# Gated one-hot rows for eight tokens: eight narrow comparison-and-product operations, or one wide comparison and one wide product

## The chip, the cores and the metric

The kernel runs on one core of a Trainium2 chip. The metric is the device time of one execution in microseconds. A core has TensorE (matmuls), VectorE, ScalarE and GpSimd (elementwise work, each with its own queue of instructions), and SyncE, whose queue issues most of the DMA transfers. The engines wait for each other through semaphores.

## The reference, cut to what matters

The program is two transformer blocks in a row, each over two layers and 256 tokens of width 1024. The first block ends each layer with a mixture of 16384 small experts. An expert has a number of two parts, `i1 * 128 + i2`, and each token picks 8 heads x 16 experts, with a softmax gate for each:

```python
eidx = jnp.take_along_axis(cidx, pos, axis=-1)       # 8 x 16 experts of each token
gate = jax.nn.softmax(top, axis=-1).astype(h.dtype)
u = expert_u[ec]
act = jax.nn.gelu(jnp.einsum('td,thkd->thk', hc, u), approximate=False)
return jnp.einsum('thk,thkd->td', gc * act, expert_v[ec])
```

## The kernel before

The kernel does not gather experts. It streams all of them and weights each token's activation of each expert by a gate, which is zero for those that the token did not pick. For that it needs a table `G` of gates: for each token a 128 x 128 matrix, first key by second key. The table is built in the loop that is changed here.

For one token, the 128 picks lie across the partitions of `pairsT`: `pairsT[:, 0]` is one part of the expert's number, `pairsT[:, 1]` the other, `pairsT[:, 2]` the gate, each with one column for a token. `iota` holds 0 to 127 along the free dimension of every partition. Comparing `iota` with a pick's part gives a one-hot row of 128. The product of the plain one-hot rows (part 1) and the gated ones (part 0, multiplied by the gate), summed over the 128 picks by one matmul, is the token's 128 x 128 gate matrix.

Tokens go in groups of `TOKG = 8`, 32 groups in each of two layers. `rows` holds two groups, `[:, n % 2, 0]` gated and `[:, n % 2, 1]` plain, all f32 in SBUF. For a group n:

- VectorE (L2328 to L2337) makes the eight gated rows, one `tensor_scalar` each, which compares and multiplies (L2331), and the last of the plain rows (L2335), and signals `gated_rows`.
- GpSimd (L1947 to L1953) makes four plain rows (L1951) and signals `plain_rows`.
- ScalarE (`one_hot`, L1650 to L1657) makes three plain rows as relu(1 - (key - iota)^2): three squares (L1653), a drain, one relu over all three (L1655), and signals `act_rows`.
- TensorE (L1126 to L1134) waits for the three signals, and for the copy of group n - 2, then multiplies eight times (L1132) into one half of `gate_ps` and signals `gates_full`.
- ScalarE (`gates_out`, L1661 to L1663) copies the group's gates from PSUM to `G` and signals `gates_kept`. Its order is rows of group n + 1, then the copy of group n.

VectorE, GpSimd and ScalarE each begin the rows of group n when TensorE has finished group n - 2 (`gates_full.two_before`), since its buffer is then free. After the loop the experts are streamed, which needs the whole of `G`. In the first layer VectorE runs L2322, a subtraction of two SBUF tensors of 2048 elements per partition, just before the loop, when GpSimd has already begun its rows. Other lines that are read below: L1392 and L1400 belong to the picking of the keys ahead of the loop (`pick_keys`, on VectorE and on GpSimd), L1408 and L2314 to L2318 to the softmax of the gates, L1930 to the inverse roots of the norms, L2013 to a norm, and L2344 to the stream of experts.

Of the kernel before, what the change touches and what calls it, by code (L numbers as in the profile page):

```python
# [11 lines left out]
ALU = mybir.AluOpType  # L12
# [3 lines left out]
P = 128  # L16
# [16 lines left out]
TOKG = 8  # L33
# [114 lines left out]
def spread(ap, axis, n):  # L148

    v = ap.unsqueeze(axis)  # L150
    shape = list(v.shape)
    shape[axis] = n
    return v.broadcast_to(shape)
# [65 lines left out]
def two_blocks(nc, io, out):  # L219
    ctx = ExitStack()  # L220
    with ctx:
        def sem(name):
            return ctx.enter_context(nc.semaphore(name))

        def sb(name, shape, dt=F32):
            return ctx.enter_context(nc.sbuf_tensor(name, shape, dt))
# [57 lines left out]
        gated_rows = Signal(sem("gated_rows"), a=S // TOKG)  # L284
# [41 lines left out]
        iota = sb("iota", [P, P])  # L326
# [110 lines left out]
        rows = rs.take(2, 2, TOKG, P)  # L437
        rp = Region(arena, NKEYS * S + D + 2 * S + 2 * KD * S)
        pairsT = rp.take(3, S)
# [77 lines left out]
        def acc_nat(b, n=512):  # L517

            return acc[:, b].rearrange("p (t x) s -> p t (x s)", t=2)[:, :, 0:n]
# [1440 lines left out]
        def _(dve_):  # L1960
            dve = nc.vector
# [192 lines left out]
            for l in range(DEPTH):  # L2154
# [171 lines left out]

                for n in range(S // TOKG):
                    dve.wait_ge(*gates_full.two_before("a", l, n + 1))  # L2328
                    for q in range(TOKG):
                        tok = n * TOKG + q  # L2330
                        dve.tensor_scalar(rows[:, n % 2, 0, q, :], iota[:], pairsT[:, 0, tok:tok + 1],  # L2331
                                          pairsT[:, 2, tok:tok + 1], ALU.is_equal, ALU.mult)
                    for q in range(POOLQ + ACTQ, TOKG):
                        tok = n * TOKG + q
                        ins = dve.tensor_scalar(rows[:, n % 2, 1, q, :], iota[:], pairsT[:, 1, tok:tok + 1], None,  # L2335
                                                ALU.is_equal)
                    ins.then_inc(gated_rows.sem, 1)  # L2337

                dve.wait_ge(*gates_kept.at("a", l, S // TOKG))

# [82 lines left out]
            for l in range(DEPTH):  # L2423
# [45 lines left out]
                for t in range(T):  # L2469
                    ins = dve.scalar_tensor_tensor(bt2[:, t], cc[:, t, 0:QR], rstd[:, t:t + 1], cqg, ALU.mult, ALU.mult)  # L2470
                ins.then_inc(qk_ready.sem, 1)
                for t in range(T):
                    ins = dve.scalar_tensor_tensor(bt[:, t, 0:KVR], cc[:, t, QR:QR + KVR], rstd[:, T + t:T + t + 1], ckvg,
                                                   ALU.mult, ALU.mult)
# [15 lines left out]
                for t in range(T):  # L2490
                    ins = dve.tensor_tensor(oh[:, t], oh[:, t], spread(subln, 1, DH), ALU.mult)
# [20 lines left out]
                for t in range(T):  # L2512
                    dve.tensor_copy(kf4[:, t, :, 0:NOPE], kv4[:, t, :, 0:NOPE])
                    ins = dve.tensor_copy(kf4[:, t, :, NOPE:LQ], spread(cc[:, t, 384:416], 1, LH))
# [18 lines left out]
                for c in range(NB):  # L2533
                    for n in range(GC):
# [6 lines left out]
                        for t in range(T):  # L2541
                            ins = dve.scalar_tensor_tensor(bt[:, t], gcol[:, t], 1.0, acc_nat(accs.buf("b", use))[:, t],
                                                           ALU.add, ALU.mult)
                        ins.then_inc(accs.free_sem("b", use), 1)
                        dve.drain()
                        for t in range(T):
                            if c == 0:
                                ins = dve.tensor_scalar(bn[:, t, cols], bt[:, t], 0.5, None, ALU.mult)
                            else:
                                ins = dve.scalar_tensor_tensor(bn[:, t, cols], bt[:, t], 0.5, bn[:, t, cols], ALU.mult, ALU.add)  # L2550
# [167 lines left out]
```

## Time and profile before

| what | value |
|---|---|
| median of 3 runs | 3237.7 us (3234.63 to 3239.08) |
| the profiled execution, its own time | 3236.21 us |
| its span, first to last instruction | 3234.3 us |
| busy: TensorE matmul, VectorE, ScalarE, GpSimd | 92%, 60%, 39%, 8% of the span |
| mean granted TensorE clock | 0.959 |
| the changed loop, layer 0 | VectorE's first operation at 294.3 us, TensorE's last eight matmuls end at 380.2 us |
| the changed loop, layer 1 | 1389.96 us to 1475.9 us |

Shares of the span are averages over stages with different limits; the loop is about 170 us of it. An idle engine costs time only where the next thing waits for it. The granted clock is 1 at TensorE's full level (2.4 GHz) and 0.5 at the lower one (1.2 GHz); a value between them is a mixture over the stretch.

### The profile page before, as it was taken

Reading aid. Unit: us, or ns where it says so; the run is one execution under the profiler, and the core shown is the slowest. Engines: PE = TensorE matmul, PEld = TensorE weight load, DVE = VectorE, ACT = ScalarE, POOL = GpSimd, SP = SyncE. Lnnn points to the kernel's source line nnn. Section 1 sums busy time; section 2 is a strip of 40 time slices with the busy share of each in tenths; the row PEclk is TensorE's granted clock in tenths of the full one; section 3 lists DMA queues with packets and bytes.
Section 4 is the critical chain, followed back from the end, with each engine's and each line's share of the span. In section 5 each row is a group of like instructions: output and inputs, shape, how many; then the busy total and the mean of one; then the engine's idle time right before and its main releaser. Section 6 shows DMA issues by size and latency. Waiting matters only on the chain.

```text
span 3234.3 us, 48577 instructions
## 1 busy us (share of the span) xinstructions
PE 2989.4 (92%) x17170; PEld 2544.4 (79%) x17170; DVE 1949.9 (60%) x3622; ACT 1276.4 (39%) x2037; POOL 274.2 (8%) x387
## 2 busy tenths in 40 slices
PE   8897899999999888968999999998999898999898
PEld 4574798999999765867999999987874887975597
DVE  4659856777777632897666666655542654543464
ACT  0235744444444311575444444434430433431243
POOL 0027600000000000572000000000000000000000
PEclk9899999999999988989999999998999999999899
DMA  8432155666666531304555555544332454323353
GB/s 314 181 118 79 43 189 205 228 229 233 230 225 231 189 122 52 118 1 142 184 188 188 193 196 190 194 158 178 114 142 104 158 188 165 119 117 124 130 183 143
DMA packets 130819, 524.25 MB, mean 162 GB/s; under 512 B 17997, under 2 KB 28109, under 8 KB 108041
## 3 DMA queue, kind: packets, MB, share of 16 engines
q1 hardware_dynamic: 120664, 508.13, 44.5%
q10 hardware_dynamic: 10034, 14.52, 1.3%
q8 instruction: 74, 1.21, 0.2%
q14 instruction: 47, 0.39, 0.0%
HBM read 519.44 MB, written 3.16 MB: 162 GB/s over the span
## 4 chain that ended last, share of the span: by engine, by line
PE 77%; issue 8%; ACT 6%; DVE 6%; DVEq 1%; ACTq 1%; DMA 1%; POOL 0%; PEldq 0%; SPq 0%; POOLq 0%; PEld 0%
PE prob_ps L1149 22%; PE acc L1160 21%; PE acc L858 7%; PE acc L798 4%; PE acc L843 3%; PE acc L819 3%; PE acc L1341 3%; PE acc L1356 3%; PE acc L1317 3%; ACT arena L1663 2%; PE turn_ps L926 2%; PE turn_ps L871 1%; PE acc L900 1%; ACT arena L1653 1%; ACT slab L1655 1%
## 5 line engine op out<-in xcount | busy, mean ns | idle before, releaser
L1149 PEld LDWEIGHTS prob_ps<-hTr,utr 128*128 128x128 f32 x5952 | 749.2, 192 | 33.1 <-issue 15.0
L1149 PE MATMUL prob_ps<-hTr,utr 128*128 128x256 f32 x5952 | 760.4, 284 | 8.3 <-DVE arena L2392 3.5
L1160 PE MATMUL acc<-vr,wtr 128*128 128x512 f32 x3024 | 736.4, 392 | 5.2 <-DVE vr L2369 5.2
L1160 PEld LDWEIGHTS acc<-vr,wtr 128*128 128x128 f32 x3024 | 553.8, 189 | 111.4 <-issue 6.4
L2369 DVE TENSOR_TENSOR vr<-slab,vr 128x1024 fp32r<-128x1024 f32 x252 | 308.7, 1225 | 418.1 <-ACT vr L1697 418.0
L1697 ACT CAST vr<-slab 128x1024 fp32r<-128x1024 f32 x252 | 264.5, 1050 | 586.7 <-PE acc L1160 584.1
L2344 DVE TENSOR_TENSOR utr<-slab,utr 128x1024 fp32r<-128x1024 f32 x248 | 302.0, 1218 | 14.0 <-ACT utr L1680 14.0
L1680 ACT CAST utr<-slab 128x1024 fp32r<-128x1024 f32 x248 | 259.3, 1046 | 9.5 <-issue 4.9
L1930 POOL TENSOR_TENSOR small<-small 128x2 f32<-128x2 f32 (+3 forms) x18 | 24.4, 1355 | 2798.3 <-DVE small L2002 1488.2
L2583 DVE TENSOR_TENSOR slab_lo<-slab,w_hi 128x2048 fp32r<-128x2048 f32 x64 | 143.8, 2288 | 126.2 <-ACT w_hi L1903 126.2
L1687 ACT ACTIVATE arena<-prob_ps 128x256 f32<-128x256 f32 x248 | 95.4, 385 | 225.3 <-PE prob_ps L1149 225.3
L1903 ACT CAST w_hi<-slab 128x2048 fp32r<-128x2048 f32 x64 | 119.3, 1906 | 164.8 <-DMA slab<-in_pack_b 151.6
L2431 DVE TENSOR_TENSOR slab_r<-slab,arena_r 128x2048 fp32r<-128x2048 f32 (+1 forms) x52 | 115.7, 2258 | 110.3 <-ACT arena_r L1777 86.8
L1132 PE MATMUL acc<-slab 128*128 128x128 f32 x1024 | 133.9, 286 | 41.2 <-ACT slab L1655 30.6
L1132 PEld LDWEIGHTS acc<-slab 128*128 128x128 f32 x1024 | 123.9, 198 | 51.5 <-DVE slab L2335 41.9
L819 PE MATMUL acc<-hT,slab 128*128 128x256 f32 x704 | 159.2, 386 | 1.7 <-issue 1.7
L1356 PE MATMUL acc<-w_hi,uTr 128*128 128x512 f32 x512 | 157.9, 390 | 2.5 <-issue 2.3
L1951 POOL TENSOR_SCALAR slab<-iota,arena 128x128 f32<-128x128 f32 x256 | 153.9, 616 | 45.1 <-ACT arena L1377 29.2
L2331 DVE TENSOR_SCALAR slab<-iota,arena 128x128 f32<-128x128 f32 x512 | 152.5, 367 | 3.6 <-PE acc L1132 3.4
L819 PEld LDWEIGHTS acc<-hT,slab 128*128 128x128 f32 x704 | 135.6, 194 | 22.3 <-issue 3.7
L871 PE MATMUL turn_ps<-ident,arena 128*128 128x128 f32 (+1 forms) x336 | 68.2, 365 | 91.8 <-ACT arena L1757 41.6
L871 PEld LDWEIGHTS turn_ps<-ident,arena 128*128 128x128 f32 (+1 forms) x336 | 51.9, 185 | 113.4 <-ACT arena L1757 33.4
(272 smaller groups left out, 4054.1 us busy)
## 6 DMA issues: line engine op xcount, KB each, us to landing
slab<-in_pack_b SPq DMA_DIRECT2D x132, 1024.0 KB, 4.8
slab<-in_peer_v SPq DMA_DIRECT2D x256, 512.0 KB, 3.5
slab<-in_peer_u SPq DMA_DIRECT2D x248, 512.0 KB, 4.7
arena<-in_pack_a SPq DMA_DIRECT2D x84, 512.0 KB, 5.4
slab<-in_pack_a SPq DMA_DIRECT2D x40, 1024.0 KB, 6.8
arena<-in_peer_u SPq DMA_DIRECT2D x4, 1024.0 KB, 13.0
slab<-in_pack_b SPq DMA_DIRECT2D x4, 832.0 KB, 5.3
arena<-in_pack_a SPq DMA_DIRECT2D x2, 1024.0 KB, 18.7
```

The costliest lines, as they stand in the source:

```text
L819: ins = pe.matmul(dst, w(k, a, P), lhs[:, k, :], start=(k == 0), stop=(k == KD - 1))
L858: ins = pe.matmul(dst[:, t, 0:n], hT_r[hp][:, 4 * h + k, t * P:t * P + P], proj_operand(u0 + h, wp)[:, k, a:a + n], start=(h == 0 and k == ...
L1132: ins = pe.matmul(gate_ps[:, n % 2, q * P:q * P + P], rows[:, n % 2, 1, q, :], rows[:, n % 2, 0, q, :], start=True, stop=True)
L1149: ins = pe.matmul(prob_ps[:, m % 2, 0:S], utr[:, m % 2, uh, k * P:k * P + P], hTr[:, hh, k, :], start=(k == 0 and n == 0), stop=(k == KD - ...
L1160: ins = pe.matmul(y_ps[:, t, n, :], wtr[:, m % 2, wh, t * P:t * P + P], v_place(l, i)[:, vh, n * 512:n * 512 + 512], start=first and k == ...
L1356: ins = pe.matmul(dst[:, t, :], uTr[:, up, 4 * j + k, t * P:t * P + P], mlp_operand(u, wp)[:, k, :], start=(j == 0 and k == 0 and m == 0), ...
L1680: act.copy(utr[:, m % 2, 0], expert_u[:, m % 2]).then_inc(ut_act.sem, 1)
L1697: act.copy(v_place(l, i)[:, 0], expert_v[:, m % 2]).then_inc(v_hi.sem, 1)
L1951: ins = nc.gpsimd.tensor_scalar(rows[:, n % 2, 1, q, :], iota[:], pairsT[:, 1, tok:tok + 1], None, ALU.is_equal)
L2331: dve.tensor_scalar(rows[:, n % 2, 0, q, :], iota[:], pairsT[:, 0, tok:tok + 1], pairsT[:, 2, tok:tok + 1], ALU.is_equal, ALU.mult)
L2344: dve.tensor_tensor(utr[:, m % 2, 1], expert_u[:, m % 2], utr[:, m % 2, 0].bitcast(F32), ALU.subtract).then_inc(ut_dve.sem, 1)
L2369: dve.tensor_tensor(v_hl[:, 1], expert_v[:, m % 2], v_hl[:, 0].bitcast(F32), ALU.subtract)\
```

## The change

VectorE makes the eight gated rows of a group with two operations in place of eight. The first compares 8 x 128 elements: the picks' parts of eight tokens, each repeated 128 times, with `iota`, repeated eight times. `spread` makes a view with a step of zero along one axis; nothing is copied. The second multiplies the result in place with the eight gates, each repeated 128 times. Between the two stand the one plain row of VectorE, as before, and a drain. The signal `gated_rows` moves from L2335 to the product. GpSimd's, ScalarE's and TensorE's parts are unchanged.

```diff
                 for n in range(S // TOKG):
                     dve.wait_ge(*gates_full.two_before("a", l, n + 1))
-                    for q in range(TOKG):
-                        tok = n * TOKG + q
-                        dve.tensor_scalar(rows[:, n % 2, 0, q, :], iota[:], pairsT[:, 0, tok:tok + 1],
-                                          pairsT[:, 2, tok:tok + 1], ALU.is_equal, ALU.mult)
+                    first, gated = n * TOKG, rows[:, n % 2, 0]
+                    dve.tensor_tensor(gated, spread(pairsT[:, 0, first:first + TOKG], 2, P), spread(iota[:], 1, TOKG),
+                                      ALU.is_equal)
                     for q in range(POOLQ + ACTQ, TOKG):
-                        tok = n * TOKG + q
-                        ins = dve.tensor_scalar(rows[:, n % 2, 1, q, :], iota[:], pairsT[:, 1, tok:tok + 1], None,
-                                                ALU.is_equal)
-                    ins.then_inc(gated_rows.sem, 1)
+                        tok = first + q
+                        dve.tensor_scalar(rows[:, n % 2, 1, q, :], iota[:], pairsT[:, 1, tok:tok + 1], None, ALU.is_equal)
+                    dve.drain()
+                    dve.tensor_tensor(gated, gated, spread(pairsT[:, 2, first:first + TOKG], 2, P), ALU.mult)\
+                        .then_inc(gated_rows.sem, 1)
```

## Rows read from the trace of the kernel before

**Rows 1.** The page: busy time of each engine over the span.
```profile
PE 2989.4 (92%) x17170; PEld 2544.4 (79%) x17170; DVE 1949.9 (60%) x3622; ACT 1276.4 (39%) x2037; POOL 274.2 (8%) x387
```

**Rows 2.** Windows: us busy of PE, PEld, DVE, ACT, POOL; granted clock, DMA share, GB/s.
```profile
294.00:300.00 6.00, 2.92 (x14) 2.95 (x15) 5.16 (x19) 1.21 (x4) 4.19 (x7) 0.50 0.00 0
300.00:310.00 10.00, 8.36 (x61) 7.88 (x61) 9.12 (x33) 8.40 (x17) 8.37 (x15) 0.89 0.01 2
320.00:340.00 20.00, 15.71 (x126) 14.42 (x125) 20.00 (x72) 18.85 (x41) 18.55 (x32) 1.00 0.01 2
1380.00:1390.00 10.00, 1.80 (x6) 1.00 (x6) 8.02 (x17) 0.69 (x2) 0.40 (x1) 0.54 0.00 1
```

**Rows 3.** Timeline of one group: start, length, engine, line, operation, idle before it.
```profile
326.17 0.52 ACT L1655 ACTIVATE slab<-arena 128x384 f32<-128x384 f32 x1
326.20 0.31 DVE L2335 TENSOR_SCALAR slab<-iota,arena 128x128 f32<-128x128 f32 x1
326.45 2.39 DVE L2331 TENSOR_SCALAR slab<-iota,arena 128x128 f32<-128x128 f32 x8
326.62 2.38 POOL L1951 TENSOR_SCALAR slab<-iota,arena 128x128 f32<-128x128 f32 x4 [0.18 <-PE acc L1132]
...
326.95 2.02 PE L1132 MATMUL acc<-slab 128*128 128x128 f32 x16 [0.54 <-ACT slab L1655]
...
328.76 0.31 DVE L2335 TENSOR_SCALAR slab<-iota,arena 128x128 f32<-128x128 f32 x1
329.01 0.34 DVE L2331 TENSOR_SCALAR slab<-iota,arena 128x128 f32<-128x128 f32 x1
```

**Rows 4.** The chain that ended last, one turn of it in the loop.
```profile
313.97 1.01 ACT arena L1663
...
315.93 0.52 ACT slab L1655
...
316.53 1.01 ACT arena L1663
```

**Rows 5.** Waits from 304 to 378 us, and L1951 by itself (least, median, most).
```profile
PE acc L1132 <- ACT slab L1655: 15.3, 28, 0.8
...
L1951 POOL TENSOR_SCALAR slab<-iota,arena x256: 592/597/2542, 291.5 to 1472.7; 128x128 f32<-128x128 f32 x128
```

**Rows 6.** Groups of VectorE by form: count, busy time, mean ns.
```profile
L2344 DVE TENSOR_TENSOR utr<-slab,utr 128x1024 fp32r<-128x1024 f32 x248 | 302.0, 1218 | 14.0 <-ACT utr L1680 14.0
L1392 DVE TENSOR_TENSOR arena<-arena,small 128x512 f32<-128x512 f32 x8 | 5.2, 693 | 0.3
```

**Rows 7.** Timeline of VectorE: around a drain, and nine operations in a row.
```profile
289.81 0.41 DVE L2314 TENSOR_REDUCE small<-arena 128x16 f32<-128x256 f32 x1
290.30 0.25 DVE L2316 RECIPROCAL small<-small 128x16 f32<-128x16 f32 x1
...
296.80 2.26 DVE L2331 TENSOR_SCALAR slab<-iota,arena 128x128 f32<-128x128 f32 x8
```

**Rows 8.** Timeline where VectorE and GpSimd meet, and GpSimd's L1930 alone.
```profile
272.55 3.27 DVE L1400 TENSOR_TENSOR arena<-arena 128x512 f32<-128x512 f32 x2
273.56 1.71 POOL L1400 TENSOR_TENSOR arena<-arena 128x512 f32<-128x512 f32 x1
291.92 2.28 DVE L2322 TENSOR_TENSOR hTr<-hT,hTr 128x2048 fp32r<-128x2048 f32 x1
292.13 2.54 POOL L1951 TENSOR_SCALAR slab<-iota,arena 128x128 f32<-128x128 f32 x1
1270.98 0.69 POOL L1930 TENSOR_TENSOR small<-small 128x2 f32<-128x2 f32 x1 [91.68 <-DVE small L2000]
2189.54 1.22 DVE L2013 TENSOR_TENSOR arena<-x,arena 128x1024 f32<-128x1024 f32 x1
2189.72 1.62 POOL L1930 TENSOR_TENSOR small<-small 128x2 f32<-128x2 f32 x1 [716.41 <-DVE small L2002]
```

**Rows 9.** The chain that ended last, at the loop's first group.
```profile
297.08 3.77 PE acc L1132 x16
```

## The prediction

> **What bounds the kernel now.** I read the page first. Matmuls run through 92% of the span and VectorE through 60% [rows 1], so an edit to VectorE's work should matter only in a stage where TensorE waits. The edited loop is such a stage: it runs for 32 groups of eight tokens in each of two layers, and the next stage needs all of its output. The stretches [rows 2] show what the reader should look for: in the middle of the loop TensorE is busy 15.7 of 20 us, while VectorE is busy 20.00, ScalarE 18.85 and GpSimd 18.55. Three engines are nearly full, so which of them sets the pace has to be read from one group.
>
> The timeline of one group [rows 3] repeats every 2.56 us (VectorE's first narrow operation of a group starts at 326.45, of the next at 329.01). ScalarE goes copy, three squares, relu, and the copy again without waiting. VectorE does its nine operations in 2.56 us. GpSimd does four in 2.38 us and waits 0.18 us. TensorE needs 2.02 us and waits 0.54 us for ScalarE's relu: that ended at 326.69 (326.17 + 0.52), VectorE's last operation of the same group at 326.51, and TensorE began at 326.95. The chain of waits says the same [rows 4]: it stays on ScalarE, from a copy at 313.97 over the relu at 315.93 to the next copy at 316.53, 2.56 us, and touches neither VectorE nor GpSimd. The waits of the stage [rows 5] agree: 28 waits of TensorE for ScalarE's L1655 in 74 us. So ScalarE sets 2.56 us by itself; VectorE ends 0.18 us ahead of it, and GpSimd's 0.18 us of waiting is all the room that it has. Two things follow. A faster VectorE gains nothing, and nearly all that VectorE or GpSimd loses shows in the time, once per group.
>
> **The change, part by part.**
>
> *Removed*: eight narrow operations, 2.31 us from the first to the start of L2335 (326.45 to 328.76) [rows 3]. They do comparison and product in one pass.
>
> *Added on VectorE*: two operations over 1024 elements per partition. The nearest rows are two-input f32 operations of that size, 1.22 us (L2344, 1218 ns) [rows 6]. That a comparison with repeated operands costs the same is seen at half the size: L1392, whose operands are both spread in this way and which compares, takes 693 ns for 512 elements; if the row of 1024 is 1218, each further 512 elements cost 525 ns, which is 1.03 ns an element and leaves 0.17 us fixed, with no extra for the repeated operands [rows 6]. L2335 stays (0.30 us). The drain costs about 0.07 us: L2314 ends at 290.22 and the drained L2316 starts at 290.30 [rows 7]. Operations without a drain between them overlap by 0.07 to 0.08 us (eight of 0.33 us fit in 2.26 us) [rows 7]. From the comparison's start to the product's start: 1.22 - 0.07 + 0.30 + 0.07 = 1.52 us; one whole group: 1.52 + 1.22 - 0.07 = 2.67 us. VectorE alone therefore goes from 2.56 to 2.67 us, and would pass ScalarE by 0.11 us. That is the small part.
>
> *Moved*: the signal to TensorE now hangs on the product, not on L2335. TensorE waits for the last of all operations in both kernels, so this adds nothing beyond the 2.67 us.
>
> *GpSimd*: its four one-hot rows (L1951) run beside VectorE's. What a wide two-input VectorE operation does to a GpSimd operation in flight is visible in two places [rows 8]. L1951 itself takes 0.597 us (the median; least 0.592, most 2.542) [rows 5], but the one that began at 292.13, beside the 2.28 us L2322, took 2.54 us; L2322 ended at 294.20, the GpSimd operation 0.47 us later. L1930 takes 0.69 us alone and 1.62 us beside L2013 (1.22 us); it ended 0.58 us after L2013. In both cases the GpSimd operation did its first 0.12 us (0.597 - 0.47, 0.69 - 0.58), then stood still until the wide operation ended, then did the rest. So each wide operation costs GpSimd the time from its next attempt to the wide operation's end. GpSimd's operations follow each other every 0.577 us (four in 2.38 us with the last one 0.597 and the first 0.05 longer), so this lies between 1.22 - 0.58 = 0.64 and 1.22 us. A narrow VectorE operation has no such price: nine of them and four of GpSimd's share 2.56 us, though one after the other they would need 2.56 + 2.38 us [rows 3].
>
> The bounds for a group are then 2.36 + 2 x 0.64 = 3.64 us and 2.36 + 2 x 1.22 = 4.80 us, where 2.36 us is GpSimd's group undisturbed. Between them I walk through two groups, with these prices and 2.06 us from the last arrival to TensorE's end. Let GpSimd and VectorE be done with group n at 0, VectorE already with n+1. GpSimd does n+1 undisturbed until 2.36. TensorE frees group n's buffer at 2.06, so VectorE compares for n+2 from 2.10 to 3.32: GpSimd's first operation of n+2 starts at 2.36, is held at 2.48 and ends at 3.80. Its second wants to read at 3.90, in the product (3.62 to 4.84), and ends at 5.32. TensorE ended n+1 at 4.42, so VectorE goes on with n+3 (comparison to 6.12, product 6.45 to 7.67); GpSimd's third operation ends at 6.60, its fourth at 8.15. Then VectorE has n+3 done and the pattern begins again: two groups in 8.15 us, 4.07 us each. It lies inside the bounds because some wide operations fall where GpSimd has just been, and it is the value that I take.
>
> The Trainium skill has the rule behind this, SBUF — State Buffer, section "Who interferes with whom": a VectorE instruction with two SBUF inputs contends with a GpSimd instruction that reads SBUF, and the later one waits for the whole of the first. By that rule, read strictly, GpSimd's operations would hold VectorE as long too, and a group would be the sum of the two, 4.80 us; the rows show GpSimd's first 0.12 us overlapping, so the sum by the rows is 4.07. The rule in its strict form is the first rival below.
>
> *The sum*: 31 steps from group to group in each of two layers, 62 in all, by 4.07 - 2.56 = 1.51 us: 93.6 us. The profiled execution took 3236.2 us (span 3234.3, 1.9 us around it), 1.5 us under the median of 3237.7, so it stands for the median, and I add to that: 3237.7 + 93.6 = 3331.3 us.
>
> *Taken as nothing*: DMA, busy at a share of 0.00 and 0.01 in the loop [rows 2], and ScalarE's 2.56 us, which now fits in 4.07. TensorE's clock was at its lower level (granted 0.50) when the loop began, after a stretch in which TensorE had been busy 1.80 of 10 us at a granted 0.54, and at the full level with 15.71 of 20 busy [rows 2]. The new loop, at 2.02 of 4.07 us, lies between these rows. At half clock the first eight matmuls took 3.77 us from 297.08 on [rows 9], and that still fits beside 4.07. Only the next stage would begin slow. Of this one's stretch from 300 to 310 a granted 0.89 leaves 2.2 us at the lower level [rows 2], so the full level came at 302.2, 5.1 us after TensorE's first matmul; half of that is lost, 2.5 us a layer. I take 0 and keep 5 us for the upper end.
>
> **The rivals.**
>
> *Strict turns.* GpSimd's operations hold VectorE as fully as VectorE's hold them: 2 x 1.22 + 2.36 = 4.80 us a group, + 62 x 2.24 = 139 us, 3377 us. For it: in the key picking two L1400 of VectorE took 3.27 us instead of 2 x 0.69, beside GpSimd's own L1400 (1.71 us) [rows 8]. Against it: that one reads two tensors of 512, L1951 one of 128, and the walk leaves VectorE idle enough to wait.
>
> *VectorE alone.* GpSimd's holds do not add up, because VectorE runs ahead into GpSimd's idle moments; the group is 2.67 us, at most 2.85 with a stall in it: + 7 to 18 us, 3245 to 3256 us. Against it: GpSimd has only 0.18 us idle of 2.56, and 2.44 of 2.67 us would be wide operations.
>
> *Not slower.* The one mechanism is ScalarE's cover: if a wide operation takes no more than 1.165 us (2 x 1.165 + 0.37 - 0.14 = 2.56) and GpSimd is not held, ScalarE's 2.56 us still ends last and the time stays 3237.7 us. A gain is excluded by the same chain, unless ScalarE gets faster. All rows of that size lie at 1.22 us [rows 6], and both held operations [rows 8] speak against it. The Trainium skill, VectorE: DVE Perf Modes, section on the TRN2 errata, advises tiles of 512 elements or more since each instruction pays a fixed latency once; by that advice alone the loop would shrink, and the result would be this rival's.
>
> **How the numbers follow.** Held GpSimd as walked 0.73, strict turns 0.12, VectorE alone 0.10, not slower 0.05. The time is that of the likeliest, 3331 us. Its own bounds are 3.64 and 4.80 us a group, 3305 and 3377 us with no clock loss. The ends of 3.64 and 4.80 need every wide operation to meet GpSimd at its best or its worst moment, which seldom happens; to hold 8 in 10 over all cases I go from 3288 (3.37 us a group, some of the holds hidden) to 3372 us (4.73 us, or 4.65 and 5 us of clock). A measurement of this kernel tells 0.2% (6.5 us) from no change. Slower 0.94, same 0.045 (with the low edge of VectorE alone), faster 0.015.
>
> **What would show it.** Right: L1951's mean above 0.9 us with single ones of 1.1 to 1.8 us; TensorE waiting for GpSimd's L1951, where it waited for ScalarE's L1655; VectorE waiting for TensorE before the wide comparison; two wide operations of 1.22 us; ScalarE's copies about 4 us apart, perhaps short and long in turn (2.4 and 5.8). Wrong: TensorE waits for VectorE's product, L1951 at 0.6 us, a group of 2.7 us; or wide operations well over 1.22 us, which would mean that GpSimd holds VectorE. The prediction fails most easily in how often a wide operation meets GpSimd, since only the price of one meeting is read from rows.

## The result, and the profile after

The changed kernel takes 3391.5 us (3388.7 to 3393.7), the kernel before 3236.6 us in the runs beside it: a ratio of 1.048, 95% interval 1.046 to 1.050, 155 us slower. The prediction had the sign and the first cause; 3331 us and its range up to 3372 us were too low.

The page of the changed kernel, busy time of each engine, then VectorE's and GpSimd's groups of the loop and the one for TensorE's matmuls:

```profile
PE 3036.3 (90%) x17170; PEld 2594.0 (77%) x17170; DVE 1954.9 (58%) x3238; ACT 1276.1 (38%) x2037; POOL 399.8 (12%) x387
...
L1132 PE MATMUL acc<-slab 128*128 128x128 f32 x1024 | 179.5, 356 | 153.5 <-POOL slab L1951 153.5
...
L1951 POOL TENSOR_SCALAR slab<-iota,arena 128x128 f32<-128x128 f32 x256 | 279.4, 1108 | 72.9 <-PE acc L1132 46.9
...
L2330 DVE TENSOR_TENSOR slab<-arena,iota 128x1024 f32<-128x1024 f32 x64 | 78.2, 1222 | 140.4 <-PE acc L1132 140.2
```

VectorE's busy time has hardly moved (1949.9 to 1954.9 us, [rows 1]). GpSimd's has grown by 126 us, all in L1951, whose mean went from 616 to 1108 ns with the same 256 operations. TensorE now waits 153.5 us for it. The comparison is 1222 ns, as priced.

The same lines singly (least, median and most in ns), to be read against L1951 in [rows 5]:

```profile
L1951 POOL TENSOR_SCALAR slab<-iota,arena x256: 592/597/2687, 293.3 to 1625.7; 128x128 f32<-128x128 f32 x128
L2330 DVE TENSOR_TENSOR slab<-arena,iota x64: 1215/1222/1227, 296.0 to 1620.2; 128x1024 f32<-128x1024 f32 x64
L2336 DVE TENSOR_TENSOR slab<-slab,arena x64: 1224/1225/1228, 297.6 to 1621.7; 128x1024 f32<-128x1024 f32 x64
```

None of the 128 wide operations took over 1.228 us: L1951 never lengthened one, and between these two the holding goes one way. (The narrow plain row between the two wide ones is another matter: L2334 takes 0.40 us at 326.00, where a held GpSimd operation ends beside it, and 0.28 us in the run with operands in PSUM below.)

The timeline of the changed loop, two groups, answers to [rows 3]. The pattern repeats every 10.24 us (324.86 to 335.10), 5.12 us a group where it was 2.56:

```profile
324.86 1.22 DVE L2330 TENSOR_TENSOR slab<-arena,iota 128x1024 f32<-128x1024 f32 x1 [4.75 <-PE acc L1132]
325.03 1.53 POOL L1951 TENSOR_SCALAR slab<-iota,arena 128x128 f32<-128x128 f32 x1 [1.56 <-PE acc L1132]
326.47 1.22 DVE L2336 TENSOR_TENSOR slab<-slab,arena 128x1024 f32<-128x1024 f32 x1
326.53 2.68 POOL L1951 TENSOR_SCALAR slab<-iota,arena 128x128 f32<-128x128 f32 x1
327.62 1.22 DVE L2330 TENSOR_TENSOR slab<-arena,iota 128x1024 f32<-128x1024 f32 x1
329.14 1.23 DVE L2336 TENSOR_TENSOR slab<-slab,arena 128x1024 f32<-128x1024 f32 x1
329.20 1.63 POOL L1951 TENSOR_SCALAR slab<-iota,arena 128x128 f32<-128x128 f32 x1
330.81 2.90 POOL L1951 TENSOR_SCALAR slab<-iota,arena 128x128 f32<-128x128 f32 x5
...
335.10 1.23 DVE L2330 TENSOR_TENSOR slab<-arena,iota 128x1024 f32<-128x1024 f32 x1 [4.74 <-PE acc L1132]
```

VectorE runs two groups one behind the other, four wide operations. Three GpSimd operations begin beside them and take 1.53, 2.68 and 1.63 us; the next five take 0.6 each. The one of 2.68 us spans a product and the comparison after it. And the chain of waits, against [rows 4]:

```profile
325.03 1.64 POOL slab L1951 x2
326.66 2.54 issue
329.20 2.22 POOL slab L1951 x2
331.42 0.09 issue
331.51 3.57 PE acc L1132 x16
335.08 0.02 issue
335.10 0.02 POOLq L1948
335.12 0.15 issue
335.27 1.53 POOL slab L1951
```

ScalarE has left the chain. It goes: GpSimd's four rows of group n (325.03 to 331.42), TensorE's eight matmuls of n (3.57 us; the trace holds two records for each, hence x16), release, GpSimd's rows of n + 2. The reader should see the 3.57: before, a group of eight took 2.02 us [rows 3]. The stretches say why, against [rows 2] (columns as there):

```profile
320.00:340.00 20.00, 10.70 (x64) 10.37 (x64) 10.21 (x13) 9.52 (x20) 16.88 (x17) 0.83 0.00 1
340.00:360.00 20.00, 10.69 (x64) 10.36 (x64) 10.23 (x13) 9.25 (x20) 16.89 (x17) 0.83 0.00 1
1500.00:1520.00 20.00, 11.37 (x64) 11.04 (x64) 10.69 (x12) 9.66 (x20) 17.26 (x17) 0.76 0.00 0
```

TensorE's clock is granted 0.83 (layer 1: 0.76) where it was 1.00, a mixture of its two levels; TensorE stands idle 4.9 us of each 10.24, and the group after that idle time takes 3.57 us, near the 3.77 us of a group at a granted 0.50 ([rows 9], [rows 2]) and far from 2.02: it runs mostly at 1.2 GHz.

### The profile page after: what moved, and what is told of

Read it like the earlier page. It is cut to its first block, busy times and chain, and to the rows that moved or that the text cites. A ratio compares the mean times of both kernels' runs of the same rounds, so it can differ in the third digit from the quotient of the medians.

```text
span 3389.5 us, 48257 instructions
## 1 busy us (share of the span) xinstructions
PE 3036.3 (90%) x17170; PEld 2594.0 (77%) x17170; DVE 1954.9 (58%) x3238; ACT 1276.1 (38%) x2037; POOL 399.8 (12%) x387
## 4 chain that ended last, share of the span: by engine, by line
PE 77%; issue 9%; DVE 5%; POOL 4%; ACT 2%; DVEq 1%; DMA 0%; PEldq 0%; ACTq 0%; POOLq 0%; SPq 0%; PEld 0%
PE prob_ps L1149 21%; PE acc L1160 21%; PE acc L858 6%; PE acc L798 4%; POOL slab L1951 4%; PE acc L1132 4%; PE acc L1341 3%; PE acc L819 3%; PE acc L843 3%; PE acc L1356 3%; PE acc L1317 2%; PE turn_ps L926 2%; PE turn_ps L871 1%; PE acc L900 1%; PE prob_ps L911 1%
## 5 line engine op out<-in xcount | busy, mean ns | idle before, releaser
L1930 POOL TENSOR_TENSOR small<-small 128x2 f32<-128x2 f32 (+3 forms) x18 | 24.4, 1355 | 2799.9 <-DVE small L2002 1490.6
L1132 PE MATMUL acc<-slab 128*128 128x128 f32 x1024 | 179.5, 356 | 153.5 <-POOL slab L1951 153.5
L1132 PEld LDWEIGHTS acc<-slab 128*128 128x128 f32 x1024 | 174.3, 270 | 158.9 <-issue 154.6
L1951 POOL TENSOR_SCALAR slab<-iota,arena 128x128 f32<-128x128 f32 x256 | 279.4, 1108 | 72.9 <-PE acc L1132 46.9
L2330 DVE TENSOR_TENSOR slab<-arena,iota 128x1024 f32<-128x1024 f32 x64 | 78.2, 1222 | 140.4 <-PE acc L1132 140.2
```

The source lines that it names most:

```text
L1132: ins = pe.matmul(gate_ps[:, n % 2, q * P:q * P + P], rows[:, n % 2, 1, q, :], rows[:, n % 2, 0, q, :], start=True, stop=True)
L1951: ins = nc.gpsimd.tensor_scalar(rows[:, n % 2, 1, q, :], iota[:], pairsT[:, 1, tok:tok + 1], None, ALU.is_equal)
```

## The experiments

Three questions: is it the second SBUF input that holds GpSimd, does TensorE's clock belong to the sum, and what is the operation of 2.68 us worth? Two runs with less work on GpSimd then test the readings of both kernels, and two versions use what was found.

### Operands in PSUM: the hold goes away

```diff
+                iota_ps = turn_ps[:, turns.buf("a", "pairs1"), S:S + P]
+                dve.tensor_copy(iota_ps, iota[:])
...
-                    dve.tensor_tensor(gated, spread(pairsT[:, 0, first:first + TOKG], 2, P), spread(iota[:], 1, TOKG),
+                    dve.tensor_tensor(gated, spread(pairsT[:, 0, first:first + TOKG], 2, P), spread(iota_ps, 1, TOKG),
...
-                    dve.tensor_tensor(gated, gated, spread(pairsT[:, 2, first:first + TOKG], 2, P), ALU.mult)\
+                    dve.tensor_tensor(gated, gated, spread(turn_ps[:, turns.buf("a", "pairs1"), first:first + TOKG], 2, P), ALU.mult)\
```

> The changed kernel, with iota read from PSUM by the comparison and the gates read from PSUM by the product: each wide operation now has one input in SBUF and one in PSUM, same sizes, same output. Theory A (a wide VectorE operation holds up a GpSimd operation in flight only because both its inputs lie in SBUF): L1951 back to 0.60 us, a group of 2.6 to 2.8 us set by VectorE's own 2.67, the whole 3237 to 3256 us. Rival B (any wide VectorE operation that writes SBUF holds GpSimd): L1951 still 1.1 us in the mean, 3370 to 3395 us. Rival C (GpSimd plays no part, the loop waits for something else that the wide operations bring, such as TensorE's clock): no change from 3391 us.

Measured: 3242.8 us, ratio 1.0017 (1.0007 to 1.0027). L1951 and the comparison of this kernel, and its timeline:

```profile
L1951 POOL TENSOR_SCALAR slab<-iota,arena x256: 596/601/2543, 292.9 to 1482.1; 128x128 f32<-128x128 f32 x128
L2332 DVE TENSOR_TENSOR slab<-arena,turn_ps x64: 1214/1214/1222, 295.8 to 1480.6; 128x1024 f32<-128x1024 f32 x64
...
344.50 2.36 POOL L1951 TENSOR_SCALAR slab<-iota,arena 128x128 f32<-128x128 f32 x4 [0.26 <-PE acc L1132]
344.73 1.22 DVE L2332 TENSOR_TENSOR slab<-arena,turn_ps 128x1024 f32<-128x1024 f32 x1
...
347.35 1.21 DVE L2332 TENSOR_TENSOR slab<-arena,turn_ps 128x1024 f32<-128x1024 f32 x1
```

The wide operations are of the same size and length, only the place of one input differs, and the loss of 155 us shrinks to 6. Four GpSimd operations take 2.36 us again. (The 2543 is the one beside L2322 ahead of the loop, which is unchanged.) The group is 2.62 us: VectorE's own price, worked out as 2.67. Theory A holds, B and C fall.

### One of the two operations

The changed kernel with the product's gates from PSUM alone (the last pair of lines above).

> The changed kernel with half of the dose: the product reads the gates from PSUM, the comparison still reads both inputs from SBUF, so one wide operation of a group can hold GpSimd and not two. Theory A (each wide operation with two SBUF inputs holds GpSimd once): between the kernel with none (2.62 us a group, 3243 us) and that with both (5.0 us, 3391 us), and nearer to the first since TensorE's wait becomes short enough for its clock to stay up: GpSimd's 2.36 us and one hold of 0.64 to 1.1 us make 3.0 to 3.5 us a group, 3265 to 3296 us. Rival (only two wide operations back to back do harm, one fits in GpSimd's pauses): 3237 to 3250 us.

Measured: 3282.6 us, ratio 1.0139 (1.0123 to 1.0154). First and last copy to `G` lie 105.9 us apart in layer 0 (301.41 to 407.31), 3.42 us a group where the changed kernel needs 5.01, with one GpSimd operation of 1.53 to 1.61 us in each group of four and the others at 0.6. The harm follows the number of two-SBUF operations; the second costs more than the first (3391.5 - 3282.6 = 109 us against 3282.6 - 3236.6 = 46 us). In this kernel the granted clock from 340 to 380 us is 0.96, against 0.83 in the changed one, so part of what the second adds is TensorE's clock; the next run puts a number on that.

```profile
340.00:380.00 40.00, 25.57 (x192) 23.80 (x192) 31.45 (x36) 27.90 (x59) 38.36 (x49) 0.96 0.00 1
```

### Unread matmuls while TensorE waits

```diff
+FILL = 14
...
                     ins.then_inc(gates_full.sem, 1)
+                    if n % 2:
+                        for _ in range(FILL):
+                            pe.matmul(prob_ps[:, 0, 0:P], ident[:], ident[:], start=True, stop=True)
```

> The changed kernel, with 14 matmuls that nobody reads after every second group, in the 4.9 us in which TensorE waits for GpSimd, so that its clock does not fall. Theory A1 (TensorE's group of eight is in the chain, since GpSimd may start a group only when the one two before is multiplied, and it takes 3.57 to 3.80 us at the lower clock instead of 2.02): two groups take 10.24 - 1.55 = 8.7 us, the whole 31 x 1.55 + 31 x 1.7 = 101 us less than 3391 in the extreme that the whole difference counts, and at least 48 us less once GpSimd's own second group (2.3 us) takes over: 3290 to 3343 us, nearest to 3343. Rival (TensorE's group is hidden behind GpSimd's second group, as the prediction had it): within 10 us of 3391 us, with the clock at 1.00.

Measured: 3340.9 us, ratio 1.032 (1.030 to 1.034), 50.6 us less than the changed kernel, for added work. Its stretch from 340 to 360 us, and the chain at one group:

```profile
340.00:360.00 20.00, 16.93 (x146) 16.28 (x145) 13.22 (x16) 12.11 (x26) 19.96 (x18) 1.00 0.01 2
...
345.32 2.04 PE acc L1133 x16
```

The granted clock is 1.00, the group takes 2.04 us and not 3.57, and GpSimd is busy 19.96 of 20 us: it has become the limit. Two groups take 8.71 us (2.56 and 6.15 between copies). GpSimd's eight rows take 8.69 us in the changed kernel too (325.03 to 333.72), held just as long, but there GpSimd then waits 1.56 us for TensorE, in every pair of groups. That wait is what the lower clock costs. The rival, that TensorE's group is hidden in the changed kernel as well, falls: it was in the chain, at a cost of 50 us.

### A drain between product and comparison, alone and with the matmuls

```diff
                     first, gated = n * TOKG, rows[:, n % 2, 0]
+                    dve.drain()
```

> The changed kernel, with a drain between a product and the comparison of the next group. The trace shows a GpSimd operation of 2.68 us, which spans a product and the comparison that follows it 0.07 us before the product's end. Theory G (GpSimd does not get in because the two overlap): with a gap of 0.07 us that operation ends after the product, 1.54 us, the next one is held by the comparison instead, and two groups take 0.3 to 0.6 us less, 10 to 20 us in all: 3371 to 3381 us. Rival (0.07 us of gap is not enough, or GpSimd loses anyway): L1951 still has its 2.68 us, the whole within 5 us of 3391 us.

Measured: 3391.4 us, no change. The timeline of this kernel shows theory G right on the operation and wrong on the time, and its rival the reverse:

```profile
344.42 1.23 DVE L2337 TENSOR_TENSOR slab<-slab,arena 128x1024 f32<-128x1024 f32 x1
344.48 1.63 POOL L1951 TENSOR_SCALAR slab<-iota,arena 128x128 f32<-128x128 f32 x1
345.73 1.23 DVE L2331 TENSOR_TENSOR slab<-arena,iota 128x1024 f32<-128x1024 f32 x1
...
347.41 1.63 POOL L1951 TENSOR_SCALAR slab<-iota,arena 128x128 f32<-128x128 f32 x1
...
349.14 3.77 PE acc L1132 x16
...
353.10 1.59 POOL L1951 TENSOR_SCALAR slab<-iota,arena 128x128 f32<-128x128 f32 x1 [1.75 <-PE acc L1132]
```

With 0.08 us between the product's end (345.65) and the comparison, the operation of 2.68 us is gone (1.63), as theory G says, but the next GpSimd operation meets the comparison (1.33 us), and all four rows of the group are held: 6.14 us from the first row's start to the fourth's end in place of 6.38. The 0.24 us did not reach the end: between 340 and 360 us the granted clock of this kernel is 0.67 where it was 0.83, TensorE's group takes 3.77 us and not 3.57, and GpSimd waits 1.75 us for it and not 1.56 (the line with x16 is from the chain of waits). Why the clock is lower here than in the changed kernel, no run shows.

> The changed kernel, with both the drain before each comparison and the 14 unread matmuls after every second group. If the prediction's walk failed only by the clock and by the operation that was held twice, this is the loop that it walked through: 4.07 us a group, 3331 us. If the drain alone does nothing, the result is that of the unread matmuls alone. If a third cost is missing from the account, it stays above both.

Measured: 3335.0 us, ratio 1.0298 (1.0281 to 1.0315). With the clock up the drain is worth 5.9 us. This is the loop that the prediction walked through, 3331 us; two groups take 8.46 us here, 8.15 there. Two small terms of the walk can be read against this trace:

```profile
344.01 2.02 PE L1133 MATMUL acc<-slab 128*128 128x128 f32 x16 [0.99 <-DVE slab L2341]
346.07 1.01 ACT L1667 COPY arena<-acc 128x1024 f32<-128x1024 f32 x1 [3.42 <-PE acc L1133]
346.14 1.22 DVE L2335 TENSOR_TENSOR slab<-arena,iota 128x1024 f32<-128x1024 f32 x1 [2.70 <-PE acc L1133]
...
347.75 1.23 DVE L2341 TENSOR_TENSOR slab<-slab,arena 128x1024 f32<-128x1024 f32 x1
```

GpSimd's last row of the group ends at 343.91 and the buffer is free at 346.07, 2.16 us later where the walk has 2.06, so VectorE, behind its drain, starts only 0.10 us ahead of GpSimd (346.24) and not 0.26, and the first row is held for longer. From the comparison's start to the product's there are 1.61 us where the sum has 1.52, as in the changed kernel (324.86 to 326.47).

### Less work on GpSimd, in both kernels

```diff
-                    for q in range(POOLQ):
+                    for q in range(POOLQ if n < 2 else 1):
```

> The changed kernel, in which GpSimd makes one plain row of a group and not four from the third group on (the other three rows keep what an earlier group left there, so the gates are not those of the reference). Theory A: one held operation of 1.5 to 2.7 us hides behind VectorE's 2.67 us, TensorE does not wait for GpSimd, the whole 3240 to 3256 us. Rival C (the wait is not for GpSimd's rows but comes with the wide operations themselves): stays at 3391 us.

Measured: 3245.0 us, ratio 1.0021 (1.0012 to 1.0030), with one GpSimd operation of 1.87 us in a group of 2.66 us, and TensorE waits for VectorE's product:

```profile
344.55 1.87 POOL L1951 TENSOR_SCALAR slab<-iota,arena 128x128 f32<-128x128 f32 x1 [0.79 <-PE acc L1132]
344.96 2.05 PE L1132 MATMUL acc<-slab 128*128 128x128 f32 x16 [0.61 <-DVE slab L2336]
```

The GpSimd operation is still held, and costs nothing, since it is not last.

> The kernel before, with the same cut in GpSimd's rows. ScalarE sets the pace by the prediction's reading, so less work on GpSimd gains nothing: 3233 to 3240 us and still 2.56 us a group, while VectorE's narrow operations follow each other every 0.257 us and not 0.289. Rival (GpSimd or VectorE sets the pace, through what they take from each other): VectorE's eight narrow operations and the plain row in 2.31 us let the group shrink to 2.3 to 2.5 us, 3221 to 3233 us.

Measured: 3236.7 us, ratio 0.9997 (0.9988 to 1.0006), 2.56 us a group. VectorE's eight narrow operations take 2.20 us and not 2.39, and it waits for TensorE before them, while TensorE still waits for ScalarE:

```profile
340.19 2.20 DVE L2331 TENSOR_SCALAR slab<-iota,arena 128x128 f32<-128x128 f32 x8 [0.18 <-PE acc L1132]
340.69 2.02 PE L1132 MATMUL acc<-slab 128*128 128x128 f32 x16 [0.54 <-ACT slab L1655]
```

The reading of the kernel before, that ScalarE sets the pace, holds. The run also shows what GpSimd's operations cost VectorE's narrow ones beside them: 0.2 us of 2.56.

### Two versions made from this

Wide comparisons are cheap for a row that needs no product (128 elements at 1.03 ns, 0.13 us, against 0.26 for a narrow operation), if one input is in PSUM. So: the picks of a group lie in `pairsT` as sixteen neighbours, GpSimd makes gated rows with comparison and product in one operation, VectorE compares for all rows that are left at once and multiplies its gated ones, ScalarE makes two plain rows and not three. (`picks` is the new view of `pairsT`, `last` is `2 * TOKG - ACTQ`.)

```diff
-ACTQ = 3
+ACTQ = 2
...
-                        ins = nc.gpsimd.tensor_scalar(rows[:, n % 2, 1, q, :], iota[:], pairsT[:, 1, tok:tok + 1],
-                                                      None, ALU.is_equal)
+                        ins = nc.gpsimd.tensor_scalar(rows[:, n % 2, 0, q, :], iota[:], picks[:, n, q:q + 1],
+                                                      pairsT[:, 2, tok:tok + 1], ALU.is_equal, ALU.mult)
...
+                    slots = rows[:, n % 2].rearrange("p h q k -> p (h q) k")[:, POOLQ:last]
+                    dve.tensor_tensor(slots, spread(picks[:, n, POOLQ:last], 2, P), spread(iota_ps, 1, last - POOLQ), ALU.is_equal)
+                    dve.drain()
+                    dve.tensor_tensor(gated, gated, spread(turn_ps[:, turns.buf("a", "pairs1"), first:first + TOKG - POOLQ], 2, P), ALU.mult)
```

> A version built on what the runs showed, with the whole computation. GpSimd makes four gated rows in place of four plain ones, comparison and product in one operation, VectorE compares for ten rows at once (four gated, six plain) with iota in PSUM, then multiplies its four gated rows with gates from PSUM, ScalarE makes two plain rows and not three. From rows: VectorE 0.17 + 1280 x 1.03 ns = 1.49, a drain, 0.17 + 512 x 1.03 ns = 0.70, together 2.2 us; ScalarE 2.56 less a square (0.29) and 128 elements of the relu (0.1) = 2.17 us; GpSimd 2.36 us if its operation with two scalars costs 0.597 us as that with one does. A group takes 2.36 to 2.4 us, 10 to 12 us less than before: 3225 to 3227 us. Against it: GpSimd's operation with two scalars is dearer (at 0.64 us and more the gain is gone and ScalarE's old 2.56 us is back), or TensorE's order of waits adds to the 2.36 us.

Measured: 3267.5 us, ratio 1.0089 (1.0075 to 1.0102). A miss, for the reason put down as the first against it: GpSimd's operation takes 0.84 us with two scalars (and two operations), one every 0.773 us, 3.10 us a group. VectorE and ScalarE had room to spare, so one row moves:

```diff
-POOLQ = 4
+POOLQ = 3
```

> The version before it with three gated rows on GpSimd and not four. There GpSimd's operation with two scalars followed the next every 0.773 us and set 3.10 us a group. Three take 2.32 us; VectorE compares for eleven rows (0.17 + 1408 x 1.03 ns = 1.62 us) and multiplies five (0.17 + 640 x 1.03 ns = 0.83 us), 2.45 us; ScalarE stays at 2.17 us. VectorE sets 2.45 to 2.5 us, 4 to 7 us less than the kernel before: 3230 to 3234 us. Against it: a wait of GpSimd or TensorE that adds to the 2.45 us and leaves it at 2.56 us or more, 3237 us and up.

Measured: 3228.3 us, ratio 0.9974 (0.9965 to 0.9983): 8.8 us faster than the kernel before, a little more than forecast, and 163 us faster than the changed one. Its loop, one group:

```profile
343.49 1.61 DVE L2339 TENSOR_TENSOR slab<-arena,turn_ps 128x1408 f32<-128x1408 f32 x1
343.62 1.86 PEld L1133 LDWEIGHTS acc<-slab 128*128 128x128 f32 x16 [0.56 <-DVE slab L2341]
...
345.17 0.82 DVE L2341 TENSOR_TENSOR slab<-slab,turn_ps 128x640 f32<-128x640 f32 x1
...
345.91 1.61 DVE L2339 TENSOR_TENSOR slab<-arena,turn_ps 128x1408 f32<-128x1408 f32 x1
```

VectorE sets the pace, 2.42 us from comparison to comparison (343.49 to 345.91; worked out as 2.45), and TensorE waits for its product (L2341).

## Why the prediction was wrong in size

**Right.** ScalarE sets the pace of the kernel before (less work on GpSimd changed nothing). A wide operation costs 1.22 us, VectorE's group 2.67 us (2.62 to 2.66 where it sets the pace). A wide operation with both inputs in SBUF that is running when GpSimd's starts holds it, about 0.12 us after its start and until the wide one ends: shown by moving an input to PSUM, and by the dose. TensorE waits for L1951. The pattern of two groups, one short and one long interval (2.56 and 7.68 us between ScalarE's copies; 2.4 and 5.8 were predicted).

**The step that failed** is "*Taken as nothing*", on TensorE's clock: that a group of eight at half clock, 3.77 us, "still fits beside 4.07". 4.07 was the mean of two groups. In the walk's own pattern GpSimd had the rows of group n + 1 done 2.36 us after those of n, and could start on n + 2 only when TensorE had finished n. At 2.06 us TensorE was just ahead of it; at 3.6 to 3.8 us it is 1.2 to 1.4 us late, in every second group. The trace shows that lateness as GpSimd's wait of 1.56 us in each pair of groups; GpSimd's eight rows take the same 8.69 us with the clock up or down. The clock falls with TensorE's waiting (filling the wait brings it back to 1.00), and makes the wait longer. The cost of it by the run with the unread matmuls: 50.6 us.

**Terms that were too small.** GpSimd does not get in between a product and a comparison that overlap by 0.07 us; the walk let it. By the two runs with the clock up: 5.9 us. The 2.06 us to TensorE's end, for which the prediction gives no row, measured 2.16, and the 1.52 us between comparison and product 1.61. The whole times leave 3.7 us for such things (3335.0 against 3331.3), but that is luck in part. (The three differences make up the 60.2 us between 3331.3 and 3391.5 by the way they are formed.) Between the first and the last copy to `G`, both layers together, the loop takes 158.6 us before, 311.2 after, 265.6 with the unread matmuls and 258.6 with the drain as well. So inside the loops the clock cost 45.6 us and the double hold 7.0 us, and the walk's loop took 100.0 us more than before, not 93.6: the prediction is 6.4 us short there. (Two groups took 0.31 us more than in the walk, which is 9.6 us for 62 steps; 6.4 are left because the 31 steps of a layer are sixteen short intervals and fifteen long ones, and the sum took the mean.) The other 5 us of the 50.6 lie outside the loops. The next stage does start slower without the matmuls (a granted 0.72 from 465 to 470 us, against 1.00 from 443 to 448 us with them), but no run separates that from the scatter of single executions, which is 3 to 5 us here.

**The rivals.** "Strict turns" gave 3377 us, nearer than the forecast, but by luck: its mechanism did not occur, since VectorE's wide operations were never longer than 1.228 us. "VectorE alone" is what is left when GpSimd is out of the way (3243 and 3245 us; forecast 3245 to 3256). "Not slower" fell with the 1.22 us.

**The range** was too narrow because its upper end took the clock as a constant 5 us after the loop and not as something that acts in each group. How far the clock would fall could not be read from the trace before; that it multiplies a term in the chain could.

## What to carry to other kernels

Before widening VectorE operations, look at what GpSimd runs beside them: two inputs in SBUF stopped it until the operation's end here, one in PSUM did not, and narrow `tensor_scalar` operations cost it next to nothing. Where a change makes TensorE wait for much of the loop (here 4.9 us of each 10.24), price TensorE's next work at the lower clock as well, and check whether that work now releases the buffer that the stalled engine needs. Compare a duration with the interval that it must fit in, not with the mean over a pattern.

## What the runs showed of the hardware that was not expected

- The hold is one-sided between these operations: 128 wide operations with two SBUF inputs, all 1.215 to 1.228 us beside a GpSimd operation that read SBUF; GpSimd's own took up to 2.687 us in place of 0.597. The Trainium skill, SBUF — State Buffer, section "Who interferes with whom", has whichever starts first hold the pair, the other blocked fully. The trace agrees for GpSimd as the later one. For GpSimd as the earlier one it depends on the GpSimd operation. One of 128 elements did not hold VectorE: in 114 cases of three runs (the one with the product's gates in PSUM and the two with the unread matmuls) it had begun 0.27 to 0.51 us before such a wide operation, and neither took longer (at most 0.604 and 1.227 us). One of 512 elements did: in the key picking of the kernel before, L1400 of VectorE takes 1.752 us once, and not the 0.69 of its median, where GpSimd's own L1400 had begun 0.51 us before it. Where page and measurement differ, on the short operations, the measurement decides.

```profile
L1400 DVE TENSOR_TENSOR arena<-arena x16: 684/694/1752, 265.9 to 1385.5; 128x512 f32<-128x512 f32 x16
```

- GpSimd's `tensor_scalar` of 128 elements follows itself every 0.577 us with one scalar operand and one operation, every 0.773 us with two of each.
- A VectorE operation that took one input from PSUM was as fast as with both in SBUF (1.214 against 1.222 us for 1024 elements).
